# Two-layer decoder trunk with a mixture of experts, one core: the last norm's offset brought as one row and its first product issued before the last activations are turned; three small routing steps in other places

## What is computed

```python
for l in range(DEPTH):                       # DEPTH = 2
    mix = hybrid_mixer(x, w_in[l], ..., w_out[l])
    x = layer_norm(ALPHA * x + mix, ln1_g[l], ln1_b[l])
    ffn = moe_ffn(x, router_w, router_b, moe_w1[l], moe_w3[l], moe_w2[l])
    x = layer_norm(ALPHA * x + ffn, ln2_g[l], ln2_b[l])

def route(xf, router_w, router_b):           # top group of 8, then 2 experts in it
    s = sigmoid(xf @ router_w)
    ...
    return e_idx, s_sel / s_sel.sum(-1, keepdims=True)

hb = silu(xb @ w1[e]) * (xb @ w3[e])         # one_block, 1024 -> 256
return hb @ w2[e]                            # 256 -> 1024
```

## Time and profile before

| | us |
|---|---|
| median of three runs | 1159.87 (1158.64 to 1160.63) |
| the profiled execution, its time | 1159.31 |
| its span | 1157.5 |
| PE busy | 1040.3 (90%) |
| DVE busy | 384.4 (33%) |
| ACT busy | 236.8 (20%) |
| moved by DMA | 440.75 MB, mean 381 GB/s |

### The profile page before, as it was taken

How to read it: one execution, slowest core, us unless ns; L and a number is a source line. 1 busy time by engine, 2 the same in 40 slices (tenths; PEclk the granted TensorE clock), 3 DMA queues, 4 the chain that set the end, 5 groups by cost and what they waited for, 6 DMA issues and landing times.

```text
span 1157.5 us, 19198 instructions
## 1 busy us (share of the span) xinstructions
PE 1040.3 (90%) x7546; PEld 519.1 (45%) x7546; DVE 384.4 (33%) x1093; ACT 236.8 (20%) x587; POOL 18.7 (2%) x36
## 2 busy tenths in 40 slices
PE   9999988888989988887999999989988989888888
PEld 6665753334433333333456657434433333333333
DVE  4875532222222222121268656222222222221213
ACT  1245321111111111111122543111111111111111
POOL 0010000000000000000000100000000000000000
PEclk9999999999999999999999999999999999998999
DMA  9957699999999999999995676999999999999997
GB/s 309 348 222 291 258 390 416 422 420 423 423 424 422 424 423 423 423 422 422 386 323 217 267 298 273 412 410 421 422 422 422 424 422 423 421 423 423 422 422 275
DMA packets 86029, 440.75 MB, mean 381 GB/s; under 512 B 17376, under 2 KB 36960, under 8 KB 44512
## 3 DMA queue, kind: packets, MB, share of 16 engines
q1 hardware_dynamic: 85696, 439.50, 93.9%
q0 software_dynamic: 144, 0.58, 0.1%
q10 hardware_dynamic: 144, 0.07, 0.0%
HBM read 439.07 MB, written 1.05 MB: 380 GB/s over the span
## 4 chain that ended last, share of the span: by engine, by line
PE 54%; SPq 32%; DMA 4%; DVE 4%; issue 3%; ACT 2%; POOL 0%; DVEq 0%; POOLq 0%
SPq L389 24%; PE bank L1030 9%; PE bank L662 9%; PE bank L1100 7%; SPq L399 7%; PE bank L1112 5%; PE bank L1015 5%; PE bank L788 4%; DMA w_even<-in_moe_w 3%; PE bank L1106 2%; PE bank L652 2%; DMA w_odd<-in_moe_w 2%; PE bank L1065 1%; PE bank L922 1%; SPq L514 1%
## 5 line engine op out<-in xcount | busy, mean ns | idle before, releaser
L1724 ACT ACTIVATE moe<-bank 128x512 f32<-128x512 f32 (+2 forms) x164 | 84.1, 523 | 596.6 <-PE bank L1030 337.5
L1112 PE MATMUL bank<-moe 128*128 128x512 f32 (+1 forms) x264 | 119.3, 593 | 23.7 <-DVE moe L1662 22.5
L1626 DVE COPY moe<-bank 128x512 f32<-128x512 f32 x64 | 44.2, 691 | 250.0 <-PE bank L1030 245.4
L1030 PE MATMUL bank<-w_even,moe 128*32 128x512 f32 x992 | 115.5, 610 | 11.5 <-DMA w_even<-in_moe_w 11.5
L1100 PE MATMUL bank<-w_even,moe 64*32 64x512 f32 x896 | 99.0, 590 | 18.3 <-ACT moe L1880 16.7
L1015 PE MATMUL bank<-moe,x 128*128 128x128 f32 x960 | 113.3, 277 | 1.9 <-DVE moe L1662 1.9
L1030 PE MATMUL bank<-w_odd,moe 128*32 128x512 f32 x992 | 110.6, 594 | 4.0 <-DMA w_odd<-in_moe_w 4.0
L1015 PEld LDWEIGHTS bank<-moe,x 128*128 128x128 f32 x960 | 110.6, 193 | 2.2 <-issue 2.2
L1100 PE MATMUL bank<-w_odd,moe 64*32 64x512 f32 x768 | 84.8, 590 | 15.7 <-DVE moe L1646 9.0
L1662 DVE COPY moe<-bank 128x512 f32<-128x512 f32 x32 | 22.1, 691 | 219.6 <-PE bank L1100 194.5
L1112 PEld LDWEIGHTS bank<-moe 128*128 128x128 f32 x264 | 47.2, 189 | 96.1 <-DVE moe L1662 49.0
(11 more groups left out here) (195 smaller groups left out, 904.7 us busy)
## 6 DMA issues: line engine op xcount, KB each, us to landing
w_odd<-in_moe_w SPq DMA_DIRECT2D x140, 1024.0 KB, 30.3
w_even<-in_moe_w SPq DMA_DIRECT2D x136, 1024.0 KB, 28.6
w_even<-in_moe_w SPq DMA_DIRECT2D x28, 2048.0 KB, 29.1
w_odd<-in_moe_w SPq DMA_DIRECT2D x24, 2048.0 KB, 30.3
w_even<-in_w_in SPq DMA_DIRECT2D x24, 768.0 KB, 11.6
w_odd<-in_w_out SPq DMA_DIRECT2D x4, 2048.0 KB, 13.4
w_odd<-in_moe_w SPq DMA_DIRECT2D x8, 512.0 KB, 12.3
w_even<-in_w_in SPq DMA_DIRECT2D x4, 416.0 KB, 6.8
```

The costliest lines, as they stand in the source:

```text
L1030: last = mm(bank[k % 2][BLK * q:BLK * (q + 1), :], xg[:, c, BLK * k:BLK * (k + 1)], w[:, :, c, :], start=c < 4, stop=c >= 4)
L1112: return mm(Y[t][h][:, lo - 512 * h:hi - 512 * h], scatter[:, t * P:(t + 1) * P], y_rows[:, lo:hi], start=False, stop=True, skip_group_che ...
L1626: nc.vector.tensor_copy(partial[:, k, :], bank[2 if first and k == 0 else 0][:, :]).then_inc(part_dve.sem, 1)
L1724: return fn(dst, src, ACT.Copy)
```

## The change

1. SyncE also loads `ln2_b` of the last layer as one row of 1024 numbers on one partition (4 KB), into a part of `w2_even` that the last even batch has left. It is issued after D3 and before D4, behind a wait for that batch's w2 products.
2. The three offset products use a row of ones against this row in place of the identity against 128 copies. The first of them (bank 1) stands where `keep_warm(3)` stood in the last layer, ahead of the last `turn_hidden`, and waits for the row. The other two stay behind the last rows.
3. The last `turn_hidden` of each layer writes to bank 0, not bank 1.
4. VectorE scales the gates of tile 0 (the last step of `weights(0)`) while it waits for ScalarE's exponential of tile 1, and takes the score product of tile 1 before `place(1)`, not after `iters`.
5. ScalarE reads the count after it has scaled its four chunks, not before.

```diff
+        ln2_b_row = w2_even[0:1, 2 * W2:2 * W2 + DM]
@@ sync
-                for sigs, (lo, hi) in zip(w2_last_in, LAST_COLS):
+                for i, (sigs, (lo, hi)) in enumerate(zip(w2_last_in, LAST_COLS)):
+                    if l == DEPTH - 1 and i == 2:
+                        sp.wait_ge(y2_psum.sem, (b0 + m) + (y2_psum.start + 1))
+                        plain(sp)
+                        sp.dma_start(ln2_b_row, a["ln2_b"][l:l + 1, :]).then_inc(b_row_in.sem, 16)
@@ tensor
+            def offset(n):
+                t, h, i = by_tensor[n]
+                mm(bank[i][:, :], const("ones")[0:1, :], ln2_b_row[:, h * 512:(h + 1) * 512], start=True, stop=False)
...
-                    keep_warm(3, bank[2])
-                    turn_hidden(b)
+                    if l == DEPTH - 1:
+                        pe.wait_ge(b_row_in.sem, 16)
+                        offset(0)
+                    else:
+                        keep_warm(3, bank[2])
+                    turn_hidden(b, bank[0])
...
-            after(pe, DEPTH - 1, ln_in, 32)
-            for t, h, i in by_tensor:
-                mm(bank[i][:, :], ident, ln2_gb[:, 1, h * 512:(h + 1) * 512], start=True, stop=False)
+            for n in (1, 2):
+                offset(n)
@@ vector
+                    if t == 1:
+                        scale_gates(0)
                     after(v, l, z_exp, t + 1)
...
                 weigh_scores(0)
-                weights(0)
+                sum_inverse(0)
                 scores(1)
                 select(1)
+                weigh_scores(1)
@@ scalar
-                m, b0 = start_batches(act, base, l)
+                b0 = batches_before(act, base)
...
                 scale_first(6)
                 scale_first(7).then_inc(xg_act.sem, 1)
+                m, b0 = start_batches(act, base, l)
```

More of the change, by code:

```diff
@@ L278, in program @@
         mla_w_in = Signal("mla_weights_in", 8 * 16)
-        ln_in = Signal("ln2_scales_in", 2 * 16)
+        ln_in, b_row_in = Signal("ln2_scales_in", 2 * 16), Signal("ln2_b_row_in")
         w13_in = [[Signal(f"w13_{parity}_in{k}") for k in range(NB)] for parity in ("even", "odd")]
@@ L1072, in turn_gated, with turn_hidden @@
                     last.then_inc(scT_psum.sem, 1)
-                def turn_hidden(b):
+                def turn_hidden(b, to=bank[1]):
                     hc = hn.rearrange("p (f c) -> p c f", c=2)
@@ L1077, in turn_hidden @@
                     for c in range(2):
-                        last = nc.tensor.transpose(bank[1][:, SEQ + c * P:SEQ + (c + 1) * P], hc[:, c, :], ident)
+                        last = nc.tensor.transpose(to[:, SEQ + c * P:SEQ + (c + 1) * P], hc[:, c, :], ident)
                     last.then_inc(hT_psum.sem, 1)
@@ L1529, in weigh_scores, with sum_inverse, scale_gates @@
                     link(tt(gate[:, t, :], sg[:, t, :], key[:, t, :], ALU.mult))
-                def weights(t):
+                def sum_inverse(t):
                     link(nc.vector.tensor_reduce(red[:, 2 + t:3 + t], gate[:, t, :], X, ALU.add))
                     link(nc.vector.reciprocal(red[:, 4 + t:5 + t], red[:, 2 + t:3 + t]))
+                def scale_gates(t):
                     link(ts(gate[:, t, :], gate[:, t, :], red[:, 4 + t:5 + t], 1.0 / ALPHA, ALU.mult, ALU.mult))
@@ L1600, in _ @@
                 signal(ts(iters[:, :], red[:, 1:2], float(BATCHES), float(BATCHES - 2), ALU.mult, ALU.add), routed, 1)
-                weigh_scores(1)
                 after(v, l, cols_in, 96)
@@ L1627, in batch @@
                         if first and k == 0:
-                            weights(1)
+                            sum_inverse(1)
+                            scale_gates(1)
                             weigh(0, b)
@@ L1645, in batch @@
                     v.wait_ge(hT_psum.sem, b + 1)
-                    nc.vector.tensor_copy(hT_mem, bank[1][:, SEQ:2 * SEQ]).then_inc(hT_sb.sem, 1)
+                    nc.vector.tensor_copy(hT_mem, bank[0 if last_of_all else 1][:, SEQ:2 * SEQ]).then_inc(hT_sb.sem, 1)
                     if first:
```

## The result

| | before | changed |
|---|---|---|
| median of 7 runs each, us | 1158.09 (1156.52 to 1160.63) | 1163.58 (1162.25 to 1166.50) |
| the profiled execution, its time | 1159.31 | 1164.66 |
| its span | 1157.5 | 1162.9 |

The ratio is 1.0049, with a 95% interval of 1.0037 to 1.0060: slower by more than the 0.2% that can be told from no change. The forecast was 1164.2.

The account below looks back on a forecast made before the run. Bound by unbroken weight transfers in the expert stage and, after 1104.8, nearly all by TensorE. Routing -0.85, row's wait +4.91, clock +1.5, very end -0.65 make +4.91 on 1159.31: 1164.2 us, range 1161.4 to 1167.0.

Parts of the forecast that it names:

- The first rival: Row's transfer: not held up, lands at 1136.3 before TensorE asks; 1157.8 us, not slower; chance 0.10.
- So the row lands with D3. I take 1143.0; bounds are D2's landing, 1141.5: TensorE's wait ahead of the last turn: row lands at 1143.0, bounds 1141.5 and 1144.5; last rows added +4.91 us later.
- It lands in between: Rival on the row's transfer: lands at 1139 to 1141, stall 1 to 3 us, little clock loss; 1159 to 1161.5; chance 0.05.
- without their waits for D1 and D2: 16 w2 products behind the last turn: 1.71 us in place of 1.97, within the +4.91 us.
- The clock: TensorE behind the wait for the row: granted clock falls to 0.50, costing +1.5 us, bounds 0.8 and 2.5.
- The new wait is 5.1 us, so I expect the same: TensorE ahead of the first offset product: waiting 5.1 us halves the clock, as the earlier 3.78 us wait did.
- A row of ones costs what the identity costs, since the time goes by columns: The three offset products: one row of weights takes as long as the identity, so no added time.
- the sign: Whole kernel: slower, by about 0.4%; slower by over 0.2% given 0.84.
- The end: Behind the last added rows: one offset product of three gone, final product starts sooner, -0.65 us.
- The routing: Both layers' routing steps: gates 2 x 0.15, count read 0.55, together -0.85 us, bounds -0.3 and -1.3, passed on to the end.

Follow-up runs that it names:

- e3: The changed kernel with the row issued ahead of D0, into a part of `w13_even`; 1159.52 us, ratio 1.0008 to the kernel before.
- e8: The changed kernel with the three offset products over all 128 rows, the row still between D3 and D4; 1163.09 us, ratio 1.0032 to the kernel before.
- e7: e3 with the three offset products over all 128 rows; 1158.44 us, ratio 0.9994 to the kernel before.
- e12: The changed kernel with the row issued between D1 and D2, offset products over one row; 1159.22 us, ratio 1.0004 to the kernel before.
- e10: e4 with the offset products over all 128 rows; 1161.96 us, ratio 1.0032 to the kernel before.
- e4: The changed kernel with ten dummy products of 128 columns ahead of the wait for the row; 1163.64 us, ratio 1.0047 to the kernel before.
- e9: The changed kernel with the row loaded as 16 pieces of 64 numbers, at the same place in the queue; 1166.88 us, ratio 1.0072 to the kernel before.
- e5: The kernel before with one one-row dummy product of 512 columns for the last layer's `keep_warm(3)`; 1158.51 us, ratio 0.9996.
- e2: The changed kernel with the three dummies back, the row's wait and all three offset products behind the last added rows; 1159.65 us, ratio 1.0012 to before.
- e11: e2 with the offset products over all 128 rows; 1158.25 us, ratio 0.9999 to the kernel before.
- e1: The kernel before with only the routing edits on VectorE and ScalarE; 1158.27 us, ratio 1.0000.

## Why the forecast held, and where it did not

**The cause is shown.** The row, issued between D3 and D4, comes after TensorE asks for it. Moving only its transfer gives back 4.6 us (e3), or 4.65 with the other form of product (e8 to e7); standing ahead of two transfers more gives back as much (e12). The first rival, that a 4 KB row is not held up, is out: from issue to landing it took 5.7 to 7.5 us.

**The landing was mis-sized.** "So the row lands with D3. I take 1143.0; bounds are D2's landing, 1141.5" is the step that failed. It landed at 1140.31, outside the bounds, and the idle time was 2.84 us where I had 5.1. This is one execution: at the same place in the queue the row took 5.67, 6.00, 7.26 and 7.54 us from its issue (the changed kernel, e10, e4, e8), each time landing ahead of D2, and in e8 TensorE idled for 4.70 us. That is the rival "It lands in between", to which I gave 0.05, and its time of 1159 to 1161.5 missed because the clock fell all the same. I had given little to a small transfer's passing larger ones, because the earlier trace rows showed a small one waiting. They show that it waits, and not that it waits as long as the transfer ahead of it. Cut into 16 pieces (e9) the row does what I forecast: it lands with D3, 9.09 us after its issue.

**The w2 products.** I took 1.71 us for 16 of them "without their waits for D1 and D2", half of what 16 products of another kind took at half clock. The 1.97 of before has no wait in it: the weight loads idled, but TensorE was busy throughout, as this window of before shows. In e10 they took 1.97 as well. The term was 0.26 too small.

```profile
1140.00:1141.00 1.00, 1.00 (x16) 0.24 (x8) 0.00 (x0) 0.00 (x0) 0.00 (x0) 1.00 1.09 347
```

**The clock was mis-sized the other way.** I took +1.5, bounds 0.8 and 2.5. In the profiled execution the 16 w2 products lost 1.5 us (3.46 against 1.97) and the last products 1.7 (4.53 against 2.83 in e8): 3.2. The second part is not shown for the typical run, since four other executions with the same products there have 2.83. The offset product lost nothing to the clock, 1.12 us where I had it double. The turn took 0.2 us more (0.45, where e7 and e10 have 0.24), but at a granted clock of 1.00, and e5 has the same 0.45 at full clock; so this is not the clock's.

"The new wait is 5.1 us, so I expect the same" names the wait as the one cause; there are two. In e8, with products over 128 rows, the clock fell in the wait. In e2 and e3, where TensorE does not wait for the row, it fell behind products over one row, and with the other form (e11, e7) it did not. In the changed kernel itself both stand ahead of the fall, and which of them brought it is open. The step "A row of ones costs what the identity costs, since the time goes by columns" holds for the product itself (1.05 to 1.12 us with either form at full clock) and fails for what stands behind it: e2 against e11 1.1 us, e3 against e7 1.3, e4 against e10 1.4, the changed kernel against e8 1.3, each in the same direction. Each of these is within its uncertainty; the mean of the four, 1.3, is uncertain by some 1 us, by the same intervals. So it is the four together, and the granted clock in e2, e3, e7 and e11, that show it. e5, one such product with the clock at 1.00, shows that it does not always come.

**The two errors cancel** in the profiled execution: the landing was 2.7 us too late in the forecast, the clock 1.7 too small. That the total came within 0.6 us of the median is partly luck; the mechanism and the sign are not.

**The end.** I had -0.65. The last products start 2.14 us after the last added rows, where it was 2.67 and I had 1.96; but they take 2.83 and not 2.59 where they wait for VectorE's tiles (e7, at full clock). That is -0.29 in place of -0.65.

**The routing.** The gains at their places were 0.55 and 0.36 us, as worked out. At the end of the fold the profiled execution is 0.39 us ahead of that of before; but the fold ended anywhere from 1134.5 to 1138.1 in the fourteen profiled executions, so this says nothing of the gain, and e1 can't tell its total from none. Whether they are passed on whole stays open; the forecast took that they are.

**The parts.** Against its own before, e7 has -0.4 (all parts, no stall, full clock), e10 +3.6 (the wait added, clock still full), e8 +4.2 (the clock lost in the wait), the changed kernel +5.5 (one-row products). By these medians some 4 of the 5.9 us between e7 and the changed kernel are the wait, and some 2 the clock; by the executions of e7 and e10 the wait is 3. The steps between the last three are smaller than their uncertainty, so the split is an estimate, and only that the wait is the larger part is shown.

## What to carry to other kernels

A small load that a critical product needs belongs ahead of the large ones in its queue, or into a buffer that is free early enough for that: its small size doesn't bring it in time when the queue holds 9 us of work, and two places in the order were worth 4.6 us. How a row is laid out can decide when it comes as well (e9 is 3.1 us slower than the changed kernel): ask in how many pieces it goes, not only how many bytes. When full-height products in a tight chain are replaced by thin ones that cost the same by themselves, look at the granted clock of the stretch behind them.

## What the runs showed that was not expected

- Three products with one row of weights and 512 columns each, issued without a gap, were followed by a granted clock of 0.50 from 1149.6 to 1156.5 us in e2's slowest execution. The same three with 128 rows kept 1.00 (e11). One of them was followed by a half clock in e3, and not in e5.
- The 4 KB row overtook two transfers of 512 KB that had been issued before it, by 1.7 and 3.2 us in the changed kernel; in 16 pieces it landed 0.2 us behind the second of them.
- The issue of the 4 KB row took SyncE 0.32 to 0.89 us between D3 and D4, 2.36 in 16 pieces, and 6.99 between D1 and D2.
